# A two-layer mixer and mixture-of-experts kernel: the context's half of a norm and of the query projection made earlier, and the router's logits taken from rows that are not normed yet

## What is computed

```
for l in range(2):
    h  = rms_norm(x,  norm_mix[l]) * (1 + sc1)  + sh1       # and hc from the context
    hc = rms_norm(xc, norm_mix[l]) * (1 + sc1c) + sh1c
    y, yc = even_layer(...) if l == 0 else odd_layer(...)   # h @ w_in, attention, @ w_out
    x  = x + g1 * y
    h2 = rms_norm(x, norm_ffn[l]) * (1 + sc2) + sh2
    x  = x + g2 * expert_choice_ffn(h2, router[l], w1[l], w3[l], w2[l])
    ...                                                     # in layer 0 the context too

def expert_choice_ffn(h, w_router, w1, w3, w2):
    aff = softmax(h @ w_router)                             # 16 experts
    gate, idx = top_k(aff.T, cap)                           # each expert takes its 32 best tokens
    hid = silu(xe @ w1) * (xe @ w3); ye = hid @ w2 * gate   # xe = h[idx]
    return zeros.at[idx].add(ye)
```

## Time and profile before

| | |
|---|---|
| median of 3 runs | 1971.21 us (1968.96 to 1971.29) |
| the profiled execution | 1968.6 us, span 1965.7 us, mean granted TensorE clock 0.951 |
| busy | PE 1688.0 us (86%), DVE 611.9 (31%), ACT 347.1 (18%), POOL 55.8 (3%) |
| DMA | 538.13 MB, mean 274 GB/s |

### The profile page before, as it was taken

How to read it: one execution, slowest core, us unless ns; L and a number is a source line. 1 busy time by engine, 2 the same in 40 slices (tenths; PEclk the granted TensorE clock), 3 DMA queues, 4 the chain that set the end, 5 groups by cost and what they waited for, 6 DMA issues and landing times.

```text
span 1965.7 us, 23029 instructions
## 1 busy us (share of the span) xinstructions
PE 1688.0 (86%) x9618; PEld 849.0 (43%) x9618; DVE 611.9 (31%) x1396; ACT 347.1 (18%) x852; POOL 55.8 (3%) x52
## 2 busy tenths in 40 slices
PE   6999998898999989899999889799998766665664
PEld 3744764343444674333333223255564433232322
DVE  1267839512100872421313113140533111110101
ACT  2222146203011661100000000020431000000000
POOL 1000200200010000000000000000000000000000
PEclk9999999999999999999999999999998878788887
DMA  8512339944231003499999999920336999999996
GB/s 362 213 44 86 115 152 424 418 172 182 86 119 66 21 1 129 173 419 427 427 428 428 427 427 427 428 108 27 129 126 283 428 427 426 427 426 428 427 428 260
DMA packets 39097, 538.13 MB, mean 274 GB/s; under 512 B 4330, under 2 KB 4586, under 8 KB 6612
## 3 DMA queue, kind: packets, MB, share of 16 engines
q1 hardware_dynamic: 37860, 530.80, 64.8%
q0 software_dynamic: 1136, 5.88, 0.8%
HBM read 535.61 MB, written 1.05 MB: 273 GB/s over the span
## 4 chain that ended last, share of the span: by engine, by line
PE 55%; issue 25%; DMA 13%; DVE 4%; ACT 1%; DVEq 1%; POOL 0%; SPq 0%; POOLq 0%; ACTq 0%
PE bank L605 53%; DMA mem<-in_moe 9%; DMA mem<-in_ada_w 3%; PE bank L615 2%; DMA mem<-in_w_ada 1%; DVE mem L1372 1%; DVEq L1369 1%; DMA mem<-in_w_out 1%; ACT mem L2077 0%; POOL mem L2379 0%; DVE mem L1858 0%; DVE mem L1675 0%; ACT mem L2048 0%; DVE mem L1696 0%; ACT mem L2229 0%
## 5 line engine op out<-in xcount | busy, mean ns | idle before, releaser
L605 PE MATMUL bank<-mem 128*32 128x256 f32 (+9 forms) x8802 | 1573.8, 498 | 249.7 <-DMA mem<-in_moe 165.6
L605 PEld LDWEIGHTS bank<-mem 128*32 128x32 f32 (+3 forms) x8802 | 759.4, 148 | 1006.9 <-issue 693.9
L2077 ACT ACTIVATE mem<-bank 128x512 f32<-128x512 f32 (+5 forms) x269 | 132.5, 503 | 1066.3 <-PE bank L605 733.2
L1858 DVE TENSOR_TENSOR mem<-mem,bank 128x512 f32<-128x512 f32 (+1 forms) x32 | 17.8, 557 | 495.3 <-PE bank L605 495.3
L1875 DVE TENSOR_TENSOR mem<-bank,mem 32x512 f32<-32x512 f32 (+1 forms) x128 | 71.1, 555 | 225.0 <-PE bank L605 223.7
L615 PE MATMUL bank<-mem 128*128 128x128 f32 x760 | 119.6, 284 | 19.4 <-DVE mem L1858 5.0
L615 PEld LDWEIGHTS bank<-mem 128*128 128x128 f32 x760 | 86.8, 145 | 85.1 <-issue 45.0
L1526 DVE SCALAR_TENSOR_TENSOR mem<-mem 128x256 f32<-128x256 f32 x160 | 86.9, 543 | 10.4 <-issue 0.9
L1372 DVE TENSOR_SCALAR mem<-bank,mem 128x128 f32<-128x128 f32 (+2 forms) x136 | 45.6, 406 | 25.8 <-PE bank L615 25.8
L2048 ACT ACTIVATE mem<-mem 128x1024 f32<-128x1024 f32 x18 | 18.9, 1052 | 185.3 <-DVE mem L1616 156.9
L2022 ACT ACTIVATE mem<-bank 128x256 f32<-128x256 f32 (+2 forms) x54 | 19.7, 397 | 180.2 <-PE bank L605 180.1
(11 more groups left out here) (186 smaller groups left out, 517.7 us busy)
## 6 DMA issues: line engine op xcount, KB each, us to landing
mem<-in_moe SPq DMA_DIRECT2D x192, 2048.0 KB, 35.0
mem<-in_ada_w SPq DMA_DIRECT2D x24, 2048.0 KB, 11.8
mem<-in_w_in SPq DMA_DIRECT2D x10, 2048.0 KB, 8.5
mem<-in_w_ada SPq DMA_DIRECT2D x6, 2048.0 KB, 12.3
mem<-in_even_w_in SPq DMA_DIRECT2D x6, 2048.0 KB, 9.9
mem<-in_w_out SPq DMA_DIRECT2D x4, 2048.0 KB, 10.0
mem<-in_odd_w_in SPq DMA_DIRECT2D x3, 2048.0 KB, 19.8
mem<-in_even_w_out SPq DMA_DIRECT2D x2, 2048.0 KB, 7.6
```

The lines of the kernel that those rows point to most:

```text
L605: return nc.tensor.matmul(o, lhsT, rhs, start=start, stop=stop, skip_group_check=True)
L2077: took(name, S.activation(o, i, func))
```

## The change

1. The context's rows (tiles 2 and 3) are normed while PE still works on `w_out2`. Their load from memory, which POOL issued at once with two others, now waits for the use of `w_out0` (`part_used`). Their 16 transposes (`norm_half(2, 1)`) and `ada_rows(27)` go between `w_out2` and `w_out3`. After `w_out3` come `ada_rows(28)` and the context's half of q0 to q3 (`qc0`, `qc1`: 32 products of 256 columns), and only then the transposes of the rows of `x` and `ada_rows(29)`. The later q tiles have 256 columns. On SP's list `even0` changes places with `ada2.11`; both keep their slots.
2. `project_out` makes the two column halves of a tile one after the other. Between them PE transposes the rows of the tile before, as they come from the residual sum and not normed (`raw_rows`, 8 transposes), and ACT copies them out.
3. The router's weights are multiplied by the norm's gain beforehand (`router_scale`), and the shift's share of the logits is made beforehand (`router_bias`, `router_bias_rows`). The logits of the raw rows are multiplied by `rstd` and the shift's share is added (`scaled_logits`). `norm_T(3)` and `norm_T(5)` go, with their `warm(4)`. The last tile is normed by DVE after the softmax. The first MAX8 reads PSUM, so that one copy goes.

Its core, by engine:

```diff
         for i in range(21, 23):
             chunk(f"ada{i // 12 + 1}.{i % 12}", ...)
+        chunk("even0", "even_w_in", 0, 512)
+        chunk("ada2.11", "ada_w1", 11, 512)
+        for i in range(1, 6):
             chunk(f"even{i}", "even_w_in", i, 512)
@@ PE
+            def raw_rows(l, j, b):
+                pe.wait_ge(res_done, RES_BEFORE[l] + 2 * j + b + 1)
+                t = B.open(f"rT{l}.{j}{b}", "dve" if b and j == MOE[l]["T"] - 1 else "act")
+                for q in range(4):
+                    last = tr(t.ps[:, P * q:P * q + P], xres[:, j, P * (4 * b + q):P * (4 * b + q) + P])
+                B.close(t, last)
+            def router_bias(l):
+                pe.wait_ge(router_scaled, l + 1)
+                for kt in range(KT):
+                    last = mm(t.ps[0:32, 0:2], router_sb[:, kt, :], ada_col[s][:, v, 2 * kt:2 * kt + 2], ...)
...
                 for j in range(T):
-                    o = [B.open(f"{tag}{j}{n}", "dve") for n in range(2)]
-                    for kt in range(4 * len(ws)):
-                        for n in range(2):
+                    for n in range(2):
+                        t = B.open(f"{tag}{j}{n}", "dve")
+                        for kt in range(4 * len(ws)):
...
+                        if n == 0 and j:
+                            for b in range(2):
+                                raw_rows(0 if T == 4 else 1, j - 1, b)
@@ PE, project_block1
+                    if i == 2:
+                        pe.wait_ge(ctx_xn, 2)
+                        norm_half(2, 1)
+                        ada_rows(27)
...
-            for k in range(27, 30):
-                ada_rows(k)
-            norm_T(2)
+            ada_rows(28)
+            w = use("even0")
+            for h in range(2):
+                t = B.open(f"qc{h}", "act")
+                for i in range(2):
+                    last = feature_major(t, w, P * (2 * h + i), P, SEQ, TOK, o=...)
+                B.close(t, last)
+            pe.wait_ge(xn_done, NORM_SUM[2])
+            norm_half(2, 0)
+            ada_rows(29)
@@ PE, route
-                norm_T(3 if l == 0 else 5)
...
+                raw_rows(l, J, 0)                       # J = T - 1, the last tile
+                wait_took(pe, f"rT{l}.{J - 1}1")
+                logits(f"ra{l}", 0, J, "act")
+                raw_rows(l, J, 1)
+                wait_took(pe, f"ra{l}")
+                logits_rows(f"la{l}", 0, J)
+                wait_took(pe, f"rT{l}.{J}0")
+                wait_took(pe, f"rT{l}.{J}1")
+                logits(f"rl{l}", J, T, "dve")
                 wait_took(pe, f"rl{l}")
+                logits_rows(f"lg{l}", J, T)
@@ DVE, route
+                scaled_logits(f"la{l}", 0, J)
                 ps = arrive(dve, f"rl{l}")
+                took(f"rl{l}", V.tensor_copy(lgT[:, P * J:P * T], ps[:, 0:P]))
+                arrive(dve, f"lg{l}")
+                pow_wait(f"norm{n}.{J}")
+                scaled_logits(f"lg{l}", J, T)
...
+                V.tensor_scalar(x_rows[l][:, J, :], xres[:, J, :], rstd[:, J:J + 1], None, ALU.mult).then_inc(xn_done, 1)
@@ ACT, route
+                raw_rows(J, 0)
+                take(f"ra{l}", lgT[:, 0:P * J], arrive(act, f"ra{l}")[:, 0:P * J])
+                square(J)
@@ POOL
+            pool.wait_ge(part_used, 1)
             pool.dma_start(xres[:, 2:4, :], A["ctx_2"][0]...).then_inc(ctx2_in, 16)
+            roots("norm2c", rstd[:, 2:4], meansq[:, 2:4])
             pool.dma_start(rope, A["rope_tab"]).then_inc(arena_in["rope"], 16)
```

More of the change, by code:

```diff
@@ L997, in _ @@
                 done_with(f"even{i}")
+            router_bias(0)
             w = use("even5")
@@ L1616, in residual @@
                     V.tensor_tensor(xres[:, j, cs], xres[:, j, cs], res_t[i % 4], ALU.add).then_inc(res_done, 1)
-                    if half and n is not None:
+                    if half and n in (3, 5) and j == T - 1:
+                        l = n // 4
+                        ps = arrive(dve, f"rT{l}.{j}1")
+                        took(f"rT{l}.{j}1", V.tensor_copy(raw_T[l][:, 4:8, P * j:P * j + P], ps.rearrange("p (k t) -> p k t", t=P)))
+                        dve.wait_ge(sums_done, NORM_SUM[n - 1] + j + 1)
+                        scaled(meansq[:, j:j + 1], ssq[:, j:j + 1], 1.0 / D, EPS, ALU.mult, ALU.add).then_inc(ms_done, 1)
+                    elif half:
                         dve.wait_ge(sums_done, NORM_SUM[n - 1] + j + 1)
@@ L1654, in _, with router_scale, router_bias, router_bias_rows @@
                 gains(n)
+            def router_scale(l):
+                n = 3 if l == 0 else 5
+                dve.wait_ge(arena_in[f"router{l}"], 16)
+                a = norm_a[:, NORM_A[n], :].rearrange("p (k i) -> p k i", i=2)
+                for i in range(2):
+                    last = V.tensor_tensor(router_a[i], router_sb, a[:, :, i:i + 1].to_broadcast([P, KT, 32]), ALU.mult)
+                last.then_inc(router_scaled, 1)
+            def router_bias(l):
+                ps = arrive(dve, f"rc{l}")
+                took(f"rc{l}", V.tensor_copy(router_c, ps[0:32, 0:2]))
+            def router_bias_rows(l):
+                ps = arrive(dve, f"rw{l}")
+                took(f"rw{l}", V.tensor_copy(router_b, ps[:, 0:2 * EXPERTS].rearrange("p (i e) -> p i e", e=EXPERTS)))
+            router_scale(0)
+            router_bias(0)
+            router_bias_rows(0)
             def d_max(u):
@@ L2033, in _, with squares @@
             S.activation(lam_b[:, 2:4], lam_b[:, 0:2], ACT.Exp).then_inc(lam_exp, 1)
-            def squares(n, done=None, before=0, sums_of=None):
-                for j in (2, 3, 0, 1) if n == 2 else range(NORM_TILES[n]):
-                    if n == 2 and j < 2:
+            def squares(n, done=None, sums_of=None):
+                for j in range(NORM_TILES[n]):
+                    if n == 2:
                         act.wait_ge(xn_done, NORM_SUM[0] + j + 1)
                     if done is not None:
-                        act.wait_ge(done, before + 2 * j + 2)
+                        act.wait_ge(done, 2 * j + 2)
                     if sums_of is not None:
```

149 lines of the change are left out of this document (100 added, 49 removed).

## The result

| | before | after |
|---|---|---|
| median, same chip | 1970.09 us (1968.41 to 1971.29, 4 executions) | 1952.53 us (1946.83 to 1953.6, 4 executions) |
| ratio, 95% interval | | 0.9895 [0.9876, 0.9914] |
| profiled execution | 1968.6 us, span 1965.7 | 1946.83 us, span 1944.9, mean granted clock 0.953 |

The change makes the kernel faster by about 1%. The median lies in the range, 4 us under the 1956.5 us that were forecast. By the ratio it is 0.9895 x 1971.21 = 1950.5 us (1946.8 to 1954.3 by the interval), half a microsecond under the range, and the whole interval lies under the 1956.5. Its three medians lie 17.6, 18.9 and 15.7 us under those of before beside them, 17.4 in the mean, against the 14.6 of the sum.

A forecast was written before the change was run, and what follows sets the result against it. PE was taken to bound 463 to 640 us, and the DMA stream from expert 0's first release the expert stages. Terms -7.4 - 5.9 - 4.7 + 2.4 + 1.0 = -14.6 us gave 1954.0, stated as 1956.5 us; range 1951 to 1965.

The forecast's parts named there:

- The mechanism: In the expert stages, the stage's end is set by expert 0's first release; an earlier release moves the rest with it.
- Edit 1: From w_out2's end through q and rope, context first: 53.1 us plus 0.6 in place of 61.1, gain 7.4 us, bounds 6.0 to 8.0.
- The clock: In both routers, one more stretch of half clock over small products, up to 1.6 us each; 1.0 us taken for both.
- Router, layer 0: Projection's end to first MAX8 in layer 0: 8.3 us in place of 17.1; with 2.8 for transposes, gain taken as 5.9.
- Router, layer 1: Projection's end to first MAX8 in layer 1: 7.3 us in place of 12.9; with 0.9 for transposes, gain 4.7.
- Transposes in the projection: Eight raw transposes between tile halves, three times in layer 0, once in layer 1: 0.93 us each, +2.8 and +0.93 us.
- The router's shift: Eight products of 2 columns and two of 16 per layer, all new: +2.4 us in sum, bounds 1.5 and 5.5.
- the hidden gain: Rival: the expert stream is held by something other than expert 0's release, hiding the routers' gain; 1970 us, chance 0.05.
- the late context: Rival: context's rows or even0 come late and PE waits between w_out2 and q; 1964 us, chance 0.05.
- the experts' clock: Rival: PE bounds layer 0's experts because the clock begins to swing there; slower, 1997 us, chance 0.03.
- the half clock over both routers: Rival: the clock stays down over the whole of both routers; 1964.5 us, chance 0.13.

The follow-up runs named there:

- e2: The changed kernel with edit 1 undone, so only edits 2 and 3 against the kernel before: 1959.70 us, 0.9943 [0.9932, 0.9955].
- e1: The kernel before with edit 1 alone, routers as before: 1962.79 us, 0.9957 [0.9944, 0.9969] against before.
- e4: The changed kernel unchanged, run again: 1952.50 us (1950.29 to 1956.46), 0.9908 [0.9895, 0.9921] against before.
- e9: The changed kernel unchanged, run a third time: 1953.70 us (1950.99 to 1957.31), 0.9918 [0.9898, 0.9937] against before.
- e5: The changed kernel without the five unread products warm(5) under the selection in both routers: 1955.17 us, 0.9916 [0.9901, 0.9930] against before.
- e3: The changed kernel with eight unread products ahead of layer 0's first gather, holding back expert 0's release: 1959.54 us, 0.9938 [0.9924, 0.9952] against before.
- e10: The changed kernel with the context normed and transposed first ahead of layer 1 too, second run: 1947.39 us, 0.9881 [0.9861, 0.9901] against before.
- e6: The changed kernel with two more unread products in the wait between lg and affT: 1956.75 us, 0.9919 [0.9901, 0.9936] against before.
- e11: The changed kernel with two unread products ahead of the wait for w_out0: 1953.22 us, 0.9915 [0.9898, 0.9931] against before.

## Why the prediction was right in its mechanism, and where it was off

The mechanism held in every step: the release of expert 0 came sooner, and each stage kept its length (436.8 us from release to the last landing in layer 0 before, 436.4, 437.5 and 436.9 in the three profiles of after; 434.0 in layer 1, then 434.3, 434.3, 434.6). What was off is the size: the routers and the shift's share (edits 2 and 3) were reckoned at 7.2 us, and e2, which has them alone, shows 11.7 (8.9 to 13.4). Edit 1's 7.4 us lie within what e1 shows (8.6, 6.1 to 11.0). The terms, for the three profiles of after (first, e4, e9):

| term | forecast | measured |
|---|---|---|
| edit 1 | -7.4 | -7.3, -7.3, -7.3 |
| transposes in the projection, layer 0 (first expert slab's request to the projection's end) | +2.8 | +2.5, +4.3, +4.8 |
| projection's end to release, layer 0 (34.9 before) | -8.7 | -10.8, -9.2, -9.8 |
| transposes, layer 1 | +0.9 | +0.9, +0.9, +0.9 |
| projection's end to release, layer 1 (26.9 before) | -5.6 | -6.0, -5.6, -6.1 |
| the router's shift, both layers | +2.4 | +1.3 (layer 1's part by e4 and e9, taken for the first too) |
| clock | +1.0 | in the rows above |
| sum | -14.6 | -19.4, -15.6, -16.2 |

- **Edit 1** is right to 0.1 us, alone and with the rest. The rows landed in time, `even0` too.
- **The clock** is the first step that failed. "I take 1.0 for both" routers: no extra loss is there. Layer 0's router holds 6.8 us at half clock before, and 3.4, 6.8 and 6.8 in the three profiles of after; layer 1's holds 9.2, and then 6.8, 8.4 and 6.8. The prediction says of the old stretch that it "kept 1.00 through several waits", but a second place at half clock stood there, under `warm(5)`:

```profile
815.60:819.00 3.40, 3.40 (x8) 1.51 (x5) 2.67 (x9) 0.00 (x0) 0.00 (x0) 0.50 1.03 352
```

The measured stretches from the projection's end to the release include what the clock does, and are shorter even than without that term: forecast were 8.7 + 5.6 = 14.3 us less for the two, the three profiles give 16.8, 14.8 and 15.9. The half clock of the new router starts 5.6 to 8.3 us behind the projection's end and lies in good part under the selection, where PE's products are read by nobody. e5 shows that without `warm(5)` it lasts longer and the release falls back by 1.1 to 4 us. That the loss of `warm(4)` and of 24 transposes costs nothing by itself is not shown: no run puts them back.
- **Router, layer 0**: the second step, mis-sized by 1.2 us in the mean (9.9 for 8.7). MAX8 came 7.6, 7.7 and 8.0 us behind the projection's end where 8.3 were reckoned, and from MAX8 to the release, which I left at the old 17.9 us, it takes 16.5, 18.1 and 17.1. In before a place at half clock lay in expert 0's first half (0.50). In e4, with 18.1, one lies there again (818.1 to 821.5 us); in the other two none does.
- **Router, layer 1**: right to 0.3 us in the mean. MAX8 at 7.1, 7.5 and 7.5 us against 7.3.
- **Transposes in the projection**: eight start 0.87 us ahead of the next product (784.91 to 785.78), where 0.93 was forecast; 2.5 us for three times in the first profile. In e4 and e9 this stretch has one more place of 3.4 us at half clock than in before (1.7 us of their 4.3 and 4.8). It hides a part of the error: by luck the sum is nearer to the forecast than its terms are.
- **The router's shift** is the third step: 2.4 was forecast and 1.3 came. (Its bounds, 1.5 and 5.5, do not come out of their own terms either, which give 1.4 and 5.2.) A group of after, from 590 to 600 us, has its eight products of layer 0 as 16 records:

```profile
L617 PE MATMUL bank<-mem 128*32 128x2 f32 x16 | 0.7, 172 | 0.0
```

0.7 us, and the stretch from `even3` to the first expert slab grows by 0.8, in every run that has them and in none without. In layer 1 the eight products cost nothing that shows: the first product behind them starts 21.0 us behind the first of `lat` (the first projection of layer 1), as in before. The stretch from `lat` to the first expert request of layer 1 grows by 0.5 us where it holds no half clock (106.1 before, 106.6 in e4 and e9).
- **What the range left out**: the bounds took the clock to cost something or nothing, never to give back, and places at half clock in code that does not change were in no term. By the terms the change itself is worth 17.1 us in the mean, 2.5 more than forecast, and the medians say 17.4. That the two agree so well is luck too: one profile of before stands against three of after, and single executions spread over 6 to 10 us. Behind layer 0's experts, for one, the three profiles of after take 3.6 to 3.8 us longer up to layer 1's first expert request, with 6.8 us at half clock where the one profile of before has none; whether before mostly has some there is not known.

The rivals: the hidden gain is refuted by e3, the late context by e1's 73.8 us, the experts' clock by the windows (1.00 in layer 0), the half clock over both routers by the 3.4 to 6.8 us of 24.1 to 25.7 in layer 0 and the 6.8 to 8.4 of 20.8 to 21.3 in layer 1.

## What to carry to other kernels

Where a stream of transfers bounds a stage, ask of each edit only how much sooner the stream is let go, and add up those; here the single edits add to within a microsecond or two (20.3 us in two parts, 18.9 together). Work that must wait for a norm goes last, and what is independent of it goes ahead: it was right for q, and e10 shows that it is right in the next place too. Before a difference of some us between two profiles is explained, look at the part ahead of the first changed instruction, and profile the same kernel again.

## What the hardware showed

Idle times of the same length leave the clock up in one execution and bring it down in another. Behind the wait for `w_out0`, 1.97 to 2.10 us long in twelve profiles, half clock follows in six and not in the other six. Behind 3.11 us of waiting, 16 records of 512 columns took 7.12 us in one profile of after and 8.81 in another, and the 32 transposes after them 3.71 and 5.38. Two profiled executions of one program took 1946.83 and 1956.46 us; 8.3 of the 9.6 us lie in stretches with more half clock, 1.2 do not. Products that nobody reads, under a long wait (5.92 us, e5), shorten the half clock that lies there, from 13.7 us to 3.4 or 6.8; under waits of 2 us (e6, e11) they moved the half clock or made no difference that can be measured.

Small products cost nothing that shows in one place, and their full time in another. The router's eight products of layer 1 write partitions 0 to 31 of a bank and start while the last of the sixteen records of `krope` (the projection just ahead), which write partitions 64 to 95 of another, are under way (1297.0 and 1297.4 us in the first profile of after). The two groups there:

```profile
L617 PE MATMUL bank<-mem 128*32 128x512 f32 x16 | 7.1, 594 | 0.0
L617 PE MATMUL bank<-mem 128*32 128x2 f32 x16 | 0.7, 172 | 0.0
```

The next product starts 21.0 us behind `lat` with them and without them; the same eight in layer 0, among products with 128 columns of weights, cost 0.8 with the two of 16 columns. Why, no run shows.
